# The second layer's input projections of the first block, as three passes over high and low parts

## What is computed

```python
h = _rmsnorm(x, p["norm_g"]) * (1.0 + scale[:, None, :]) + shift[:, None, :]   # 256 tokens
hc = _rmsnorm(xc, p["norm_g"]) * (1.0 + scale_c) + shift_c                      # 256 context tokens
hp = h @ p["w_in"]                                                             # 1024 -> 2720 columns
if need_ctx_out: hpc = hc @ p["w_in"]                                          # layer 0 alone
else: ctx_kv = hc @ p["w_in"][:, KV_OFF:CONV_OFF]                              # layer 1
...
glu = a[..., :CONV_W] * sigmoid(a[..., CONV_W:])      # then a depthwise convolution with 31 taps,
y = conv(glu, conv_w) + conv_b                        # then a layer norm over its 256 channels
x = x + gate * (concat([attn, conv, four, sgu]) * silu(hp[..., GATE_OFF:])) @ w_out
```

## Time and profile before

| | |
|---|---|
| median of 3 runs | 1510.7 us (1509.65 to 1514.16) |
| the profiled execution's own time | 1512.14 us |
| its span, first to last instruction | 1510.3 us |
| PE busy | 1458.7 us (97%) |
| DVE busy | 984.2 us (65%) |
| ACT busy | 703.2 us (47%) |
| DMA, mean rate | 161 GB/s |
| mean granted clock of TensorE | 0.989 of full speed |

### The profile page before, as it was taken

One profiled execution on the slowest core, in us unless ns is written; L12 is line 12 of the kernel. 1 busy time (PEld: TensorE's weight loads), 2 busy tenths in 40 slices (PEclk: granted clock), 3 DMA queues, 4 the chain that ended last, 5 costly groups with the idle time before them and its releaser, 6 DMA issues.

```text
span 1510.3 us, 22108 instructions
## 1 busy us (share of the span) xinstructions
PE 1458.7 (97%) x8133; PEld 1178.9 (78%) x8133; DVE 984.2 (65%) x1627; ACT 703.2 (47%) x1211; POOL 66.2 (4%) x91
## 2 busy tenths in 40 slices
PE   5899999989999999999999999999999999999998
PEld 3778746767854888888887888878888889788887
DVE  1589325246334777777778777777777776977776
ACT  2533236241234544456566444474444656654444
POOL 0200210020001000000010000000000001100000
PEclk9899999999999999999999999999999999999999
DMA  9622147235314565565434655456655654445562
GB/s 312 208 84 84 56 153 256 67 112 181 125 52 141 187 201 188 185 213 146 138 114 135 213 167 196 149 186 208 194 168 165 210 140 158 135 148 186 184 204 86
DMA packets 197429, 242.96 MB, mean 161 GB/s; under 512 B 4304, under 2 KB 178800, under 8 KB 197232
## 3 DMA queue, kind: packets, MB, share of 16 engines
q1 hardware_dynamic: 194272, 229.43, 47.5%
q0 software_dynamic: 2512, 10.49, 2.0%
q10 hardware_dynamic: 576, 2.10, 0.4%
HBM read 240.95 MB, written 1.05 MB: 160 GB/s over the span
## 4 chain that ended last, share of the span: by engine, by line
PE 85%; DVE 5%; DMA 4%; ACT 3%; issue 2%; POOL 0%; SPq 0%; DVEq 0%; ACTq 0%; POOLq 0%
PE bank L1698 36%; PE bank L2155 19%; PE bank L2156 10%; PE bank L1787 5%; DMA weight_ring<-in_w_in 2%; DMA weight_ring<-in_w_ada 2%; PE bank L1676 1%; PE bank L2062 1%; DVE weights_low L1299 1%; DVE input_split L1332 1%; DMA weight_ring<-in_w_ffn_up 1%; PE bank L2007 1%; ACT weights_high L841 1%; PE bank L1970 1%; PE bank L1929 1%
## 5 line engine op out<-in xcount | busy, mean ns | idle before, releaser
L1299 DVE TENSOR_TENSOR weights_low<-weight_ring,weights_high 128x1024 fp32r<-128x1024 f32 x328 | 392.8, 1222 | 135.5 <-ACT weights_high L841 135.4
L2155 PE MATMUL bank<-input_split,weights_high 128*128 128x512 f32 x1344 | 479.4, 399 | 1.3 <-DVE input_split L1332 1.0
L841 ACT ACTIVATE weights_high<-weight_ring 128x1024 fp32r<-128x1024 f32 x328 | 334.9, 1049 | 108.4 <-PE bank L1698 62.5
L2156 PE MATMUL bank<-input_split,weights_low 128*128 128x256 f32 x1344 | 377.0, 280 | 0.0
L2155 PEld LDWEIGHTS bank<-input_split,weights_high 128*128 128x128 f32 x1344 | 252.5, 188 | 65.3 <-issue 1.8
L2156 PEld LDWEIGHTS bank<-input_split,weights_low 128*128 128x128 f32 x1344 | 253.8, 189 | 3.0
L1698 PE MATMUL bank<-weights_high,hidden_high 128*128 128x512 f32 x352 | 138.0, 392 | 0.7 <-DVE hidden_low L1404 0.7
L1698 PE MATMUL bank<-weights_low,hidden_high 128*128 128x512 f32 x352 | 137.9, 392 | 0.0
L1698 PE MATMUL bank<-weights_high,hidden_low 128*128 128x512 f32 x352 | 137.0, 389 | 0.0
L906 ACT ACTIVATE silu_gate<-gate_sum 128x256 f32<-128x256 f32 x88 | 36.8, 418 | 206.0 <-DVE gate_sum L1382 203.2
L1698 PE MATMUL bank<-input_split,weights_high 128*128 128x256 f32 x640 | 117.9, 286 | 0.5 <-DVE input_split L1332 0.4
(11 more groups left out here) (320 smaller groups left out, 2131.8 us busy)
## 6 DMA issues: line engine op xcount, KB each, us to landing
weight_ring<-in_w_ffn_gate SPq DMA_DIRECT2D x44, 1024.0 KB, 5.4
weight_ring<-in_w_ffn_up SPq DMA_DIRECT2D x44, 1024.0 KB, 5.3
weight_ring<-in_w_ffn_down SPq DMA_DIRECT2D x44, 1024.0 KB, 4.9
weight_ring<-in_w_in SPq DMA_DIRECT2D x32, 1024.0 KB, 5.3
weight_ring<-in_w_ada SPq DMA_DIRECT2D x24, 1024.0 KB, 6.7
weight_ring<-in_w_out SPq DMA_DIRECT2D x16, 1024.0 KB, 4.9
weight_ring<-in_w_in SPq DMA_DIRECT2D x24, 512.0 KB, 5.1
gain_row<-in_norm_gains POOLq DMA_DIRECT2D x6, 512.0 KB, 4.1
```

The lines of the kernel that those rows point to most:

```text
L841: A(unit_in(WH, U), unit_source(U), ACT.Copy).then_inc(s_high, 1)
L1299: TTn(unit_in(WL, U), unit_source(U), unit_in(WH, U).bitcast(F32), ALU.subtract).then_inc(s_low, 1)
L2155: mm(b[:, :].rearrange("p (h n) -> p h n", h=2), unit_in(WH, U)[:, k, :], HX[:, k, :, :], start=(k == 0), stop=False, skip_group_check=True)
L2156: last = mm(b[:, 0:T], unit_in(WL, U)[:, k, :], HH[:, k, :], start=False, stop=(k == KD - 1), skip_group_check=True)
```

## The change

Layer 1 uses the three passes for 16 units through `project_split` (g 2, q 2, f 2, u 2, gate 8) and for both `v` products; `a`, `kv` and `kr` stay as they were. The functions of the split get the layer as an argument. The groups of taps of layer 0 are now those of layer 1 too. The diff, cut to its core (renamings of `split_high(u)` to `split_high(0, u)` and the like are left out):

```diff
-        FIRST_DONE = [("proj", 0) + e for e in [... "agq" ..., ("kv",), ("kr",)] + [... "fu" ...] + [("v", 3)] * 2 + [("gate", j) for j in range(8)]]
+        FIRST_DONE = [[("proj", L) + e for e in [... "agq" ..., ("kv",), ("kr",)] + [... "fu" ...] + [("v", 3 - 2 * L)] * 2 + [("gate", j) for j in range(8)]] for L in range(2)]
...
@@ ACT @@
+            def split_high(L, u):
+                act.wait_ge(*filled(first_slot(L, u)))
+                if L and u < 6:
+                    act.wait_ge(*at("y_ready", "b1", 0, 3, 1))
+                elif u >= 4:
+                    act.wait_ge(*at(*FIRST_DONE[L][u - 4]))
+                A(first_high(u), first_raw(L, u), ACT.Copy).then_inc(*done("first_high", "weight", L, u))
...
-                if L == 0:
-                    split_high(2)
-                    split_high(3)
+                split_high(L, 2)
+                if L:
+                    for c in range(KD):
+                        act.wait_ge(*at("hT_ready_act" if c % 2 == 0 else "hT_ready_dve", "b1", 1, c))
+                        A(hH[:, c, 0:T], hT[:, c, 0:T], ACT.Copy).then_inc(*done("first_high", "second_input", c))
+                split_high(L, 3)
                 for j in range(2):
                     act.wait_ge(*at("proj", L, "a", j))
...
                     A(CG[:, j, 0:nq // T, PAD:PAD + T], src, ACT.Copy).then_inc(*done("a_ready", L, j))
-                    if L == 0:
-                        split_high(4 + j)
+                    split_high(L, 4 + j)
...
                     A(sq[:, j, 0:nq], B[PB[L]["q", j]][:, 0:nq], ACT.Square).then_inc(*done("q_part_ready", L, j))
-                    if L == 0:
-                        split_high(8 + j)
+                    split_high(L, 8 + j)
...
                 A(sq[:, 2, :], B[PB[L]["kv"]][:, :], ACT.Square).then_inc(*done("kv_part_ready", L))
-                if L == 0:
-                    split_high(10)
+                split_high(L, 10)
                 act.wait_ge(*at("proj", L, "kr"))
                 A(kpart, B[PB[L]["kr"]][:, :], ACT.Copy).then_inc(*done("kr_part_ready", L))
-                if L == 0:
-                    split_high(11)
-                else:
+                split_high(L, 11)
+                if L:
                     ada_copy(*ADA_NEXT[1])
... (in the same way 12 and 13 after f, 14 and 15 after u, 16 and 17 after the Fourier copies, 18 to 21 after gates 0 to 3)
@@ DVE @@
+                split_low(L, 2)
+                if L:
+                    for c in range(KD):
+                        dve.wait_ge(*at("first_high", "second_input", c))
+                        TTn(hH[:, c, T:TT], hT[:, c, 0:T], hH[:, c, 0:T].bitcast(F32), ALU.subtract).then_inc(*done("first_low", "second_input", c))
+                for u in range(3, 6 if L else 7):
+                    split_low(L, u)
+                for n, u in ((3, 8), (3, 9), (3, 10), (0, 11), (4, 12), (4, 13)):
+                    taps(n)
+                    if L and u == 12:
+                        dve.wait_ge(*at("ada_T", 1, 10))
+                        biased(1, 16, 24, "gates_biased")
+                    split_low(L, u)
... (the rotation of the key)
-                if L == 0:
-                    taps(4)
-                    split_low(14)
-                    taps(3)
-                    split_low(15)
-                    taps(4)
-                else:
-                    taps(CONV_K)
+                taps(4)
+                split_low(L, 14)
+                taps(3)
+                split_low(L, 15)
+                taps(4)
... (the copies of v and its statistics)
-                if L == 0:
-                    taps(CONV_K)
-                    split_low(16)
-                    split_low(17)
+                taps(CONV_K)
+                split_low(L, 16)
+                split_low(L, 17)
... (18 to 21 now for both layers, at their places in layer 0)
@@ PE @@
+                hs = (hH, hL) if L == 0 else (hH[:, :, 0:T], hH[:, :, T:TT])
...
                     for k in range(KD):
-                        last = three(B[bank][:, :], lambda x: w[x][:, k, :], lambda y: hs[y][:, k, :], k == 0, k == KD - 1)
+                        if L and u == 2:
+                            pe.wait_ge(*at("first_low", "second_input", k))
+                        last = three(B[bank][:, 0:nq], lambda x: w[x][:, k, :], lambda y: hs[y][:, k, :], k == 0, k == KD - 1)
...
-                    if L == 0:
+                    if L == 0 or name not in ("a", "kv"):
                         project_split(name, j, {"g": 2, "q": 4, "kv": 6, "f": 8, "u": 10, "gate": 14}[name] + (j or 0), reader)
                         return
... (v: the branch with mm goes, both layers use three)
```

More of the change, by code:

```diff
@@ L445, in at_slot, with first_slot, first_part @@
             return sem, step(count, j, 16)
[L447 to L455, removed]
+        FIRST_DONE = [[("proj", L) + e for e in [(n, j) for n in "agq" for j in range(2)] + [("kv",), ("kr",)] + [(n, j) for n in "fu" for j in range(2)] + [("v", 3 - 2 * L)] * 2 + [("gate", j) for j in range(8)]] for L in range(2)]
+        FIRST_DONE[0] += [("wout_used", 0, s, r) for s in range(4) for r in range(2)]
+        def first_slot(L, u):
+            return WIN[L, u // 2] if u < 22 else base[("wout", 0)] + (u - 22) // 2
+        def first_part(L, u, ring):
+            w = ring[:, first_slot(L, u) % RING, :]
             if u >= 22:
@@ L680, in layer @@
                         ada_copy(*pair)
[L681 to L682 removed]
+                    split_high(0, 0)
+                    split_high(0, 1)
                 for c in range(0, KD, 2):
@@ L756, in gate_silu @@
                     A(SG[:, j, 0:nq], B[PB[L]["gate", j]][:, 0:nq], ACT.Silu).then_inc(*done("sg_ready", L, j))
-                    if L == 0 and j < 4:
-                        split_high(18 + j)
+                    if j < 4:
+                        split_high(L, 18 + j)
                 gate_silu(0)
@@ L1763, in first_two @@
                             pe.wait_ge(*at(*r))
-                        pe.wait_ge(*at("first_low", "weight", j))
-                    w = [(first_high(j), first_low(j)) for j in range(2)]
+                        pe.wait_ge(*at("first_low", "weight", 0, j))
+                    w = [(first_high(j), first_low(0, j)) for j in range(2)]
                     for k in range(KD):
@@ L1888, in layer @@
                     b = B[PB[L]["v", t]]
-                    if L == 0:
-                        pe.wait_ge(*at("first_low", "weight", 13))
-                        w = (FH[:, 0:2, :].rearrange("p u (k n) -> p k u n", k=KD), ring_low[:, n % RING, :].rearrange("p (k u n) -> p k u n", k=KD, u=2))
-                        o = b[:, 0:256].rearrange("p (u n) -> p u n", u=2)
+                    pe.wait_ge(*at("first_low", "weight", L, 13))
+                    w = (FH[:, 0:2, :].rearrange("p u (k n) -> p k u n", k=KD), ring_low[:, n % RING, :].rearrange("p (k u n) -> p k u n", k=KD, u=2))
+                    o = b[:, 0:256].rearrange("p (u n) -> p u n", u=2)
                     for k in range(KD):
-                        if L == 0:
-                            last = three(o, lambda x: hs[x][:, k, t * P:(t + 1) * P], lambda y: w[y][:, k], k == 0, k == KD - 1)
-                        else:
-                            last = mm(b[:, 0:256], hT[:, k, t * P:(t + 1) * P], cols(n)[:, k, :], start=(k == 0), stop=(k == KD - 1))
+                        last = three(o, lambda x: hs[x][:, k, t * P:(t + 1) * P], lambda y: w[y][:, k], k == 0, k == KD - 1)
                     last.then_inc(*done("proj", L, "v", t))
```

83 lines of the change are left out of this document (30 added, 53 removed).

## The result

The changed kernel took 1517.76 us (median of 20 runs, 1510.21 to 1524.02) against 1511.12 us of the kernel before (20 runs, 1507.46 to 1514.16). The ratio is 1.0049, 95% interval 1.0039 to 1.0058: slower by 0.5%. The profiled execution took 1518.08 us, its span is 1516.3 us.

A forecast was written before the change was run, and what follows sets the result against it. PE was taken to bound the kernel, without a gap in layer 1. Saving 11.4 us less stalls of 3.4, 2.1 and 5.4 gave -0.5; half clock added 1.8 and 1.0: +2.3, 1513.0 us, range 1507 to 1519.

The forecast's parts named there:

- The saving of PE: Layer 1's 18 units: three passes at 0.119 us make 2.86 us per unit, saving PE 11.4 us.
- The three stalls: PE in layer 1 waits ahead of q, the second ada transposes and conv_mean: 3.4, 2.1 and 5.4 us.
- DVE's idleness ahead of low part 8: In layer 1 DVE does three pairs of taps, then idles some 10 us until f's slot and high part.
- The clock in layer 1: PE's clock halves after the first and third stalls, costing 1.8 and 1.0 us; one after the second is absorbed.
- the sum for the whole run: Whole run: -0.5 us from saving less stalls, plus 1.8 and 1.0 of half clock, gives +2.3 us.
- behind the last gate nothing changes, so the end moves by the same: After layer 1's last gate: the last gate ends 0.5 us earlier, and the run's end moves equally.
- a clock term of 1.8 + 1.0: Half clock at q costs 1.8 us; after the third stall 1.0, with bounds 0 and 3.4.
- slower, by the clock: Rival, chance 0.29: long half-clock spells after the first and third stalls cost 3.4 us each; +6.3, 1517.0 us.
- the -0.5 that the sum gave for full clock: Whole run at full clock: 11.4 us saved less stalls of 3.4, 2.1 and 5.4; as a rival, 1510.2 us, chance 0.15.
- Faster: Faster by over 0.3%, chance 0.12: mainly the rival (0.11) that taps keep up at conv_mean, -5.9 us, 1504.8.
- no change: Whole run within 0.3%, 4.5 us, of the kernel before; chance 0.58.
- the case that had 0.30: Whole run slower by over 0.3%, chance 0.30, through longer clock spells after the first and third stalls.

The follow-up runs named there:

- warm: Changed kernel plus useless matmuls on a free bank in the waits ahead of q 0 (3) and the mean (5); layer 1 98.94 us, ratio 1.0025.
- warmq: Changed kernel with 14 tap pairs ahead of low part 8, kr and ada copies earlier, 2 useless matmuls ahead of q; layer 1 90.74 us, ratio 0.9941.
- again: The changed kernel unaltered, a second comparison against the kernel before; layer 1 100.84 us, ratio 1.0016.
- after: The changed kernel as first profiled and timed against the kernel before; layer 1 101.10 us, ratio 1.0049.
- qplain: Changed kernel with q computed as before the change (plain 32-bit products, units 4 and 5 not split); layer 1 97.52 us, ratio 1.0048.
- taps_ada: Changed kernel with 14 tap pairs ahead of low part 8 and the kr and ada copies ahead of high part 10; layer 1 92.58 us, ratio 0.9994.
- best: Changed kernel with q plain, 14 tap pairs ahead of low part 8, kr and ada copies ahead of high part 10; layer 1 90.11 us, ratio 0.9967.
- best2: Repeat of changed kernel with q plain, 14 tap pairs ahead of low part 8 and earlier kr and ada copies; layer 1 90.03 us, ratio 0.9979.
- taps: Changed kernel with 14 instead of 3 tap pairs ahead of low part 8 in layer 1; layer 1 96.23 us, ratio 0.9964.
- a control: The kernel before, unaltered, timed against itself, done twice; layer 1 98.50 and 98.45 us, ratios 0.9988 and 1.0000.
- again2: The changed kernel unaltered, a third comparison against the kernel before; layer 1 100.74 us, ratio 1.0033.
- ada: Changed kernel with ACT's copies of kr and the ada rows ahead of high part 10; layer 1 100.60 us, ratio 1.0013.

## Why the prediction was right, and where it was not

**The saving of PE** was right: 2.86 us were forecast for a unit, from 0.119 us for a pass, and 2.83 measured.

**The three stalls** were right in place, releaser and size: 3.4, 2.1 and 5.4 forecast; 3.13, 2.05 and 5.03 measured. From the start of a to the mean the forecast has 391.1 - 321.7 = 69.4 us, and 71.2 with one spell; the profile has 395.58 - 324.53 = 71.05. DVE's idleness ahead of low part 8 was forecast at some 10 us and is 11.78.

**The clock in layer 1** was right in its places, one spell on q and one around the mean; 1.8 and 1.0 us were forecast. Measured: q took 7.42 instead of 5.66, so 1.8; the mean and two gates took 2.04 + 6.17 instead of 0.86 + 5.65, so 1.7, 0.7 more than forecast, since hardly any of this spell passed while PE stood (it fell at 395.2, the mean began at 395.58). `warm` and `warmq` show that the waits are what lets it fall. That a spell behind the second wait is absorbed by the third is what `again` shows. The rule of the Trainium skill, "TensorE: Matmul & The Clock Gate", "HAM oscillation", says that a kernel whose waits for DMA come back at every step starts cold after each. It holds here in kind: the wait at q, 3.13 us behind a slot of the ring, cost its own time and 1.8 us of slow products behind it.

**Layer 1 as a whole**: +2.3 forecast, +2.5 in the profile of the change, +2.2 in the two others.

**What missed** is the sum for the whole run. The median is +6.6 us, 4.3 more than the +2.3 of the sum. The step is "behind the last gate nothing changes, so the end moves by the same", together with a clock term of 1.8 + 1.0 that counts layer 1 alone. The work outside the layer is the same; the time for which PE runs it at half clock is not.

The profile of the changed kernel is 6.0 us longer than that of the kernel before, and 2.9 of these lie ahead of layer 1. The timeline of PE there and the granted clock behind its wait:

```profile
237.74 1.53 PE L1669 MATMUL bank<-weight_ring,silu_c 128*32 128x256 f32 x16 [3.33 <-DMA weight_ring<-in_w_ada]
238.50:241.50 3.00, 3.00 (x20) 2.30 (x12) 0.00 (x0) 1.49 (x3) 0.00 (x0) 0.50 0.83 261
242.00:245.00 3.00, 3.00 (x27) 1.42 (x30) 1.60 (x3) 1.80 (x5) 0.00 (x0) 1.00 0.70 238
```

Layer 0 waits there for its "ada" slots. In the kernel before these waits were 1.19 and 0.91 us, 1.2 less in all, and the clock stayed full; the spell of 3.4 us adds 1.7, and the two make the 2.9. In `warm` and `warmq` waits of 2.95 and 3.23 us at this place were followed by 10.2 us of half clock each, and they have the latest starts of a. From the keys' products of layer 0 to the first product of its output `after` took 53.5 us, these two 56.4 and 56.7, and the eleven others, with no spell in this stretch, 50.2 to 52.2. Behind layer 1 `after` has a spell at 1194 us, behind a wait of 2.38 us at the transposes of the residual, where the kernel before waited 0.55; it lacks the one that the kernel before has at 440, and so this part is only 0.6 longer.

The timed runs have no traces, but their mean clock says the same of the whole. The 20 runs of the changed kernel lost 21.1 us to half clock by the estimate of the table, the runs of the kernel before 13.7 to 14.5 in the three later comparisons; beside the 20 runs its clock was not recorded, so that 7 rests on these. Less this loss the timed runs of the changed kernel take, in the mean, 1497.0, 1494.7 and 1497.1 us in its three comparisons, and the kernel before 1495.1 and 1497.1 beside the second and the third. So the difference without the clock is -0.4 and 0.0, near the -0.5 that the sum gave for full clock, and the term that was too small is the clock: 2.8 us forecast, some 7, 3.4 and 4.7 measured. (The estimate counts a spell in full even where it passed in waiting: among the 258 timed runs, within one kernel, a us of it goes with 0.8 us of time.) The same holds for the others. By their layer 1 alone `warm`, `qplain`, `taps_ada`, `best` and `best2` lag by 3 to 8 us, and these five lost 3.0 to 9.0 us more to half clock than the kernel before; `taps` and `warmq`, which lost no more than it, do not lag.

Such a loss is what the rival "slower, by the clock" is about, and 1517.76 is near its 1517.0. Its mechanism was another: spells of 6.9 us behind two waits of layer 1, where the profile has spells of 3.4 there and further ones elsewhere. The trace of the kernel before would have warned of them, since it has more falls than the two of the earlier trace rows: at 211.0 us, for one, the clock fell for 3.4 us behind 2.00 us of idleness. That 1517.76 lies inside the range is owed to the rival that the range took in, not to the sum.

What stays **open** is why the waits outside layer 1 grow. For `best` at 994 us they grow because PE comes early while its releaser does not; for the "ada" slots of layer 0, ahead of every changed instruction, no run shows a cause, and it may be scatter. The three longest waits there are of kernels with the split, but a control waited 2.05 us, and `again` and `again2` have their a where it was.

**The chances.** Faster was given little, and no comparison of the changed kernel came near it. For no change, with 0.58 the likeliest, the bound was 4.5 us. The measurement of 20 runs lies beyond it, in the case that had 0.30; that of `again` (+2.4 by its ratio) lies within, that of `again2` (+5.0) just beyond.

## What to carry to other kernels

A saving on the busiest engine is worth what its feeders leave of it: here 11.4 us of matmuls became +2.5 us because work put ahead of the helpers' old work made both stand still for a slot that had not landed. Where an in-order helper must wait for a transfer, put its other due work ahead of that wait, and the copies that the main engine needs ahead of the split that waits; with q left plain the change then gives 8.4 us in its layer. Of these only 3 to 5 reach the whole run, since PE, come early, waits further on and its clock falls there: compare the granted clock of the timed runs before a difference of some us is put down to the change's own work. And walk the three engines' lists by hand with durations from rows: that foretold each wait to 0.4 us, while the time of a whole run is only good to some 4 us in a kernel of this length.

## What was not expected of the hardware

Short waits cost more than their length. In layer 1 each wait that was followed by half clock had 3.4 us of it behind it, which cost about 1.7. In layer 0 two waits of about 3 us had 10.2 us behind them. The stretch from the end of layer 1 to the next block, which no kernel changes, took 61.28 or 61.29 us in eight of fourteen profiles, with one spell of 3.4 us in it, 59.59 in five without one, and 62.93 in the one where it was twice as long. Waits of 1.96 to 2.39 us between dense matmuls let the clock fall in some executions and not in others: the second wait did so in `again`, `warm`, `taps` and `qplain`, not in `after`, `again2` and `ada`. Waits of 0.4 to 1.2 us in layer 1 never did.
